# A two-layer decoder trunk on one core: last token tile by column halves, third tile's last pass on two other engines, queries ahead of values, and the values' copy ahead of an exponential

## The chip, the cores and the metric

The kernel runs on one core of a Trainium2 chip. The metric is the device time of one execution in microseconds (us), lower is better. The core has TensorE (PE in the rows; PEld is its weight load), VectorE (DVE), ScalarE (ACT), GpSimd (POOL) and the queue of SyncE (SP), which issues nearly all DMAs. The engines run side by side and wait for each other through semaphores; each engine takes its own instructions strictly in the order written.

## The reference, cut to what matters

The trunk has a layer of native sparse attention (NSA) and one of forgetting attention (FoX), each followed by a gated MLP. `x` is 512 tokens by 1024. Every sub-layer ends in a layer norm over the 1024 columns of a token:

```python
def layer_norm(x, g, b):
    mu = jnp.mean(xf, axis=-1, keepdims=True)
    var = jnp.mean(jnp.square(xf - mu), axis=-1, keepdims=True)
    y = (xf - mu) * lax.rsqrt(var + LN_EPS)
    return y * g + b
...
x = layer_norm(ALPHA * x + y, ln1_g[i], ln1_b[i])
f = conv_ffn(x, ffn_w_up[i], ffn_conv_w[i], ffn_conv_b[i], ffn_w_down[i])
x = layer_norm(ALPHA * x + f, ln2_g[i], ln2_b[i])
```

NSA projects 16 heads of queries in 4 groups. Each group has keys and values of 64 columns for a "selected" and a "window" branch, and rotary (`apply_rope`) on queries and keys, not on values. A third branch attends to 31 compressed blocks. FoX is causal attention with an additive bias, 16 heads, handled in 8 pairs.

## The kernel before, in words

Each product is made of three: both operands are split into a high and a low part, and PE does high by high, high by low and low by high. A weight chunk comes by DMA into one of four `raw` slots; ScalarE makes its high part (`hi`), GpSimd the low part (`lo`), then PE may use it.

**NSA items.** A group's projections are four items of eight steps (`kstep`): n = 4 * group + k with k = 0 keys, 1 values, 2 queries of the first head pair, 3 queries of the second. All four go through bank BP of PSUM (the eight 512-column accumulator banks `ps`), which ScalarE empties by `item_copy`. Keys and queries then pass the rotary: the SP queue swaps halves by four DMAs (`swap_halves`), GpSimd multiplies by cosine, VectorE by sine (`item_dve`), GpSimd adds, ScalarE makes the high part (`item_hi`), GpSimd the low one (`rope_lo`), and for queries the SP queue moves both into place (`move_queries`). `double_keys` copies the keys to the other partitions. Values are instead turned by PE through bank BX (`values_turn`), which compressed scores (`cmp_scores`) and compressed probabilities (`cmp_turn`) use too.

The first group's items stand in a prologue, one after another, among the last steps of the compression (`cmp_hidden`, the `vcs` copies, the first compressed softmax `cmp_mask` to `cmp_scale`). Then follow 4 groups of 32 units, u = 32 * g + v. A unit is one query block of one head and branch: scores, `unit_max` (VectorE), `unit_exp` (ScalarE), scaling (GpSimd), transpose (PE), `unit_hi` and `unit_lo` (ScalarE and VectorE), product with values. While group g runs, the items of group g + 1 are projected, one step per unit, and an item's rotary lies in the eight units behind its projection. The order is written out by hand on each engine.

**FoX.** `fox_stages` runs eight units per head pair, with the next pair's three projections between them. In the last unit ScalarE copies the next pair's values out of bank BP (`fox_value_copy`), and PE needs that bank for the pair after it.

**The end.** The down projection writes tile m (128 tokens) into banks 2m and 2m + 1, and the last four weight chunks are done tile by tile (`down_pe`). `ln_dve` and `tile_std` then do for each tile: residual in two halves (L1635), mean (L1638), squares on ScalarE over all 1024 columns (L795), square root (L798), scaled by gain (L1645), inverse (L1648), last pass in two halves (L1652). Two DMAs store each tile.

## Time and profile before

| | us |
|---|---|
| three runs, median | 1373.08 |
| lowest and highest run | 1370.35, 1373.63 |
| the profiled execution, its own time | 1374.31 |
| its span in the trace | 1372.5 |
| TensorE matmuls busy in it | 1322.0 (96%) |
| VectorE, ScalarE, GpSimd busy | 635.4, 674.6, 599.4 |

The span runs from the first to the last event of the core; some 1.8 us of the execution lie outside it. An engine's busy time says how full it is, not whether it sets the end: for that one reads who waits for whom.

### The profile page before, as it was taken

To read this page: it belongs to the slowest core of one execution; us is meant where nothing else is said; L and a number is where in the kernel's file an instruction comes from. 1 tells how busy PE (TensorE), PEld (TensorE's weight loads), DVE (VectorE), ACT (ScalarE), POOL (GpSimd) and SP (SyncE) were. 2 spreads that over 40 slices of the span, in tenths; PEclk is the share of its full clock that TensorE was granted. 3 is DMA by queue.
4 is the path that set the end of the run, shared out by engine and by line. 5 is a ranking of instruction groups with operands and counts; after the bars stand their busy time and mean duration, and the time that the engine had idled before them with its cause. 6 is when DMAs were issued, how large, how long until landed. Compare 5 with 4: busy or idle time off the path is not lost.

```text
span 1372.5 us, 19855 instructions
## 1 busy us (share of the span) xinstructions
PE 1322.0 (96%) x6858; PEld 1108.3 (81%) x6858; DVE 635.4 (46%) x1469; ACT 674.6 (49%) x1257; POOL 599.4 (44%) x399
## 2 busy tenths in 40 slices
PE   8979999979999999999999999998999999999997
PEld 6868887867898888888888788887898888888885
DVE  3347777775544433440006767768354343341005
ACT  4347777765444444442214767776354444443122
POOL 2267767763434444444444222222244444444441
PEclk9999999999999999999999999999999999999999
DMA  9442322222323333334333321322424333334321
GB/s 296 108 102 61 85 70 78 69 70 97 99 82 108 92 95 103 92 105 131 101 92 95 87 62 49 94 64 62 154 78 123 92 92 98 100 93 137 103 66 62
DMA packets 172798, 131.98 MB, mean 96 GB/s; under 512 B 24544, under 2 KB 156244, under 8 KB 172724
## 3 DMA queue, kind: packets, MB, share of 16 engines
q1 hardware_dynamic: 172724, 131.02, 33.0%
q8 instruction: 43, 0.70, 0.2%
q14 instruction: 31, 0.25, 0.1%
HBM read 117.17 MB, written 4.39 MB: 89 GB/s over the span
## 4 chain that ended last, share of the span: by engine, by line
PE 82%; DVE 5%; issue 4%; ACT 4%; POOL 2%; DMA 2%; SPq 1%; DVEq 0%; POOLq 0%; ACTq 0%
PE ps L964 15%; PE ps L965 15%; PE ps L966 15%; PE ps L1218 7%; PE ps L1221 7%; PE ps L1219 7%; PE ps L1124 3%; PE ps L1138 2%; PE ps L1091 2%; PE ps L1264 2%; PE ps L1260 2%; PE ps L1259 2%; DVE ptl L1507 1%; DVE prob L1489 1%; PE ps L1137 1%
## 5 line engine op out<-in xcount | busy, mean ns | idle before, releaser
L488 POOL TENSOR_TENSOR wl<-raw,wh 128x1024 fp32r<-128x1024 f32 x178 | 426.3, 2398 | 648.0 <-ACT wh L611 647.9
L964 PE MATMUL ps<-xh,wh 128*128 128x512 f32 x968 | 381.8, 394 | 4.2 <-ACT work L900 3.9
L965 PE MATMUL ps<-xl,wh 128*128 128x512 f32 x968 | 377.9, 390 | 0.0
L966 PE MATMUL ps<-xh,wl 128*128 128x512 f32 x968 | 377.4, 390 | 0.0
L611 ACT ACTIVATE wh<-raw 128x1024 fp32r<-128x1024 f32 x192 | 201.2, 1050 | 191.8 <-PE ps L1221 182.2
L964 PEld LDWEIGHTS ps<-xh,wh 128*128 128x128 f32 x968 | 182.2, 188 | 41.9 <-ACT work L900 5.8
L966 PEld LDWEIGHTS ps<-xh,wl 128*128 128x128 f32 x968 | 181.9, 188 | 38.8
L965 PEld LDWEIGHTS ps<-xl,wh 128*128 128x128 f32 x968 | 182.1, 188 | 33.4
L1664 DVE SCALAR_TENSOR_TENSOR work<-ps,conv,work 128x511 f32<-128x511 f32 x88 | 66.0, 750 | 222.0 <-ACT work L847 156.7
L705 ACT ACTIVATE prob<-prob,negmax 128x128 f32<-128x128 f32 x192 | 107.4, 559 | 69.4 <-DVE negmax L1489 67.5
L1218 PE MATMUL ps<-wh,gh 128*128 128x512 f32 x352 | 137.1, 390 | 0.0
L1219 PE MATMUL ps<-wl,gh 128*128 128x512 f32 x352 | 136.9, 389 | 0.0
L1635 DVE SCALAR_TENSOR_TENSOR ps<-xt,ps 128x512 f32<-128x512 f32 x32 | 21.4, 710 | 237.9 <-PE ps L1221 237.9
L1489 DVE CUSTOM_DVE_ANT_0 prob<-ps,seen 128x128 f32<-128x128 f32 x192 | 92.8, 484 | 42.7 <-PE ps L1344 29.6
L1221 PE MATMUL ps<-wh,gl 128*128 128x512 f32 x352 | 108.4, 389 | 0.0
L548 POOL TENSOR_SCALAR prob<-prob,rinv,gate 128x128 f32<-128x128 f32 (+3 forms) x128 | 78.7, 615 | 65.9 <-DVE rinv L1496 64.2
L712 ACT ACTIVATE pth<-ps 128x128 fp32r<-128x128 f32 x192 | 82.3, 429 | 43.4 <-PE ps L1124 42.2
L1507 DVE TENSOR_TENSOR ptl<-ps,pth 128x128 fp32r<-128x128 f32 x192 | 93.1, 485 | 3.9 <-ACT pth L712 3.4
L1124 PE MATMUL ps<-ident,prob 128*128 128x128 f32 x480 | 87.3, 280 | 6.4 <-POOL prob L548 3.2
L850 ACT ACTIVATE gh<-work 128x512 f32 (+1 forms) x44 | 27.8, 632 | 118.5 <-DVE work L1676 118.5
L1221 PEld LDWEIGHTS ps<-wh,gl 128*128 128x128 f32 x352 | 66.1, 188 | 13.8
L1218 PEld LDWEIGHTS ps<-wh,gh 128*128 128x128 f32 x352 | 66.1, 188 | 13.7
(197 smaller groups left out, 1948.8 us busy)
## 6 DMA issues: line engine op xcount, KB each, us to landing
raw<-in_ffn_w_up SPq DMA_DIRECT2D x88, 512.0 KB, 3.8
raw<-in_ffn_w_down SPq DMA_DIRECT2D x44, 512.0 KB, 3.6
raw<-in_fox_w_in SPq DMA_DIRECT2D x24, 512.0 KB, 4.0
raw<-in_nsa_w_in SPq DMA_DIRECT2D x12, 512.0 KB, 4.9
xt<-in_x SPq DMA_DIRECT2D x8, 512.0 KB, 5.0
raw<-in_nsa_w_in SPq DMA_DIRECT2D x16, 256.0 KB, 3.8
qs<-work SPq DMA_DIRECT2D x32, 128.0 KB, 2.3
raw<-in_nsa_w_o SPq DMA_DIRECT2D x8, 512.0 KB, 4.1
```

The source lines that it names most:

```text
L488: nc.gpsimd.tensor_tensor(wl[:, slot, :, :], raw[:, slot, :, :], wh[:, slot, :, :].bitcast(F32), ALU.subtract).then_inc(s_wl, 1)
L611: nc.scalar.activation(wh[:, slot, :, :], raw[:, slot, :, :], ACT.Copy).then_inc(s_wh, 1)
L705: nc.scalar.activation(prob[:, u % 3, 0:n], prob[:, u % 3, 0:n], ACT.Exp, bias=negmax[:, b:b + 1], scale=-1.0, accum_out=psumrow[:, b:b + ...
L964: nc.tensor.matmul(o, ah, bh, start=start, stop=False)
L965: nc.tensor.matmul(o, ah, bl, start=False, stop=False)
L966: return nc.tensor.matmul(o, al, bh, start=False, stop=stop)
L1124: last = nc.tensor.transpose(ps[:, BT + u % 2, kt * P:(kt + 1) * P], prob[:, u % 3, kt * P:(kt + 1) * P], ident[:, :])
L1218: nc.tensor.matmul(ps[:, 2 * m + h, :], a_h, hi_w[:, cs], start=start, stop=False)
L1219: nc.tensor.matmul(ps[:, 2 * m + h, :], a_h, lo_w[:, cs], start=False, stop=False)
L1221: last = nc.tensor.matmul(ps[:, 2 * m + h, :], a_l, hi_w[:, h * 512:(h + 1) * 512], start=False, stop=stop)
L1489: nc.vector.tensor_tensor_reduce(out=prob[:, u % 3, 0:n], in0=ps[:, BS + u % 2, 0:n], in1=seen[:, SEQ - n:SEQ], scale=-1.0, scalar=3e38, o ...
L1507: nc.vector.tensor_tensor(turned_blocks(ptl, i), ps[:, BT + u % 2, 0:(i + 1) * P].rearrange("p (k c) -> p k c", c=P), turned_blocks(pth, i ...
```

## The change

1. The item order within a group becomes keys, first queries, values, second queries (`KIND`); waits on counters follow it, and the values' turn, high part and low part move to units 25, 26 and 27.
2. The prologue is reordered on PE, ScalarE, VectorE, GpSimd and SP alike.
3. In FoX the values' copy stands ahead of the exponential of the same unit on ScalarE.
4. In the last layer norm the fourth tile is projected by column halves, and its variance is put together from the squares of each half about its own mean and the gap between the two means. The third tile's last pass is made by ScalarE (times the inverse) and GpSimd (plus `b_row`) in place of VectorE.

```diff
+KIND = (0, 2, 1, 3)
...
+        def rotated_ahead(n):
+            return n - (n + 1) // 4
         def queries_ahead(n):
-            return 2 * (n // 4) + max(n % 4 - 2, 0)
+            return 2 * (n // 4) + n % 4 // 2
...
-                if n % 4 == 3 or n % 4 == 0 and n:
+                if n % 4 == 2 or n % 4 == 0 and n:
                     move_queries(n - 1)
-                if n % 4 == 1:
+                if n % 4 == 1 and n > 1:
                     double_keys(n // 4)
-                else:
+                if n % 4 != 2:
                     swap_halves(n)
+                if n == 1:
+                    double_keys(0)
             def load_item(n):
-                g, k, c = n // 4, n % 4, 4 + n
+                g, k, c = n // 4, KIND[n % 4], 4 + n
                 if k >= 2:
                     load(c, c % R, cols(w_nsa, g * REP * HD + (k - 2) * P))
...
-                sp.wait_ge(s_y, 3 * QT + n + 1)
+                if m == 2:
+                    sp.wait_ge(s_yp, half + 1)
+                else:
+                    sp.wait_ge(s_y, 3 * QT + (n if m < 2 else n - 2) + 1)
...
+            for h in range(2):
+                cs = slice(h * 512, (h + 1) * 512)
+                pool.wait_ge(s_yr, h + 1)
+                nc.gpsimd.tensor_tensor(xt[:, 2, cs], xt[:, 2, cs], b_row[:, cs], ALU.add).then_inc(s_yp, 1)
...
-                    if turned and w == (3, 5, 2, 2)[item[1]]:
+                    if turned and w == (3, 2, 2, 2)[item[1]]:
                         item_hi(*item)
...
                 for v in range(8):
+                    if more and v == 7:
+                        fox_value_copy(C_FOX + 3 * (pair + 1) + 2, NSA_ITEMS + 3 * (pair + 1))
                     if more or v + 2 < 8:
                         unit_exp(U + v + 2, (v + 2) % 4)
-                    if more and v == 7:
-                        fox_value_copy(C_FOX + 3 * (pair + 1) + 2, NSA_ITEMS + 3 * (pair + 1))
...
-            for m in range(QT):
+            for m in range(QT - 1):
                 tile_std(3, m)
+            act.wait_ge(s_lt, 1)
+            act.wait_ge(s_sq, 4 * QT - 1)
+            nc.scalar.activation(swapped.bitcast(BF16)[:, 0:512], ps[:, 6, :], ACT.Square, bias=last_mean[:, 0:1],
+                                 accum_out=squares[:, 3:4]).then_inc(s_sq, 1)
+            act.wait_ge(s_rstd, 4 * QT - 1)
+            act.wait_ge(s_gz, 4 * QT - 1)
+            for h in range(2):
+                nc.scalar.activation(xt[:, 2, h * 512:(h + 1) * 512], ps[:, 4 + h, :], ACT.Identity, scale=rstd[:, 2:3],
+                                     bias=zero[:, 0:1]).then_inc(s_yr, 1)
+            act.wait_ge(s_lt, 3)
+            act.wait_ge(s_sq, 4 * QT)
+            nc.scalar.activation(swapped.bitcast(BF16)[:, 512:1024], ps[:, 7, :], ACT.Square, bias=last_mean[:, 1:2],
+                                 accum_out=second_squares[:, :]).then_inc(s_sq, 1)
+            act.wait_ge(s_lt, 6)
+            act.wait_ge(s_sq, 4 * QT + 1)
+            nc.scalar.activation(std[:, 3:4], second_squares[:, :], ACT.Sqrt, bias=last_var[:, 0:1], scale=1.0 / D).then_inc(s_std, 1)
...
-            pe.wait_ge(s_kc, 3)
-            item_steps(0)
-            conv_turn(0)
-            cmp_hidden(1)
-            pe.wait_ge(s_kc, 4)
-            item_steps(1)
-            pe.wait_ge(s_gel, 2)
-            for g in range(GROUPS):
-                for hb in range(2):
-                    last = nc.tensor.matmul(ps[0:NCMP, 4, g * HD:(g + 1) * HD], ghid[:, hb, g * NCMP:(g + 1) * NCMP], w2v[:, hb, :],
-                                            start=(hb == 0), stop=(hb == 1))
-            last.then_inc(s_cmpo, 1)
-            pe.wait_ge(s_pl, 1)
-            values_turn(0)
-            item_steps(2)
-            conv_turn(1)
...
+                    pe.wait_ge(s_pl, 4 * g + 2 + h // 2 * 2)
                     pe.wait_ge(s_qm, 64 * (2 * g + 1 + h // 2))
...
+                n = 4 * ((H + 1) // 4) + 3
+                if H and n < NSA_ITEMS:
                     pe.wait_ge(s_pl, n)
...
+                pe.wait_ge(s_pf, 4 * g + 2 + j % 2 * 2)
...
+                if not j:
+                    pe.wait_ge(s_pl, 3)
                 for i in range(QT):
...
+                if p % 16 == 0:
+                    pe.wait_ge(s_pl, 4 * g + 3)
                 pv(p, bank, vv[g % 2][:, :, br, :, :], p % 4 == 0, p % 4 == 3)
...
+            pe.wait_ge(s_kc, 3)
+            item_steps(0)
+            conv_turn(0)
+            item_steps(1)
+            cmp_hidden(1)
+            pe.wait_ge(s_kc, 4)
+            item_steps(2)
+            pe.wait_ge(s_gel, 2)
+            for g in range(GROUPS):
+                for hb in range(2):
+                    last = nc.tensor.matmul(ps[0:NCMP, 4, g * HD:(g + 1) * HD], ghid[:, hb, g * NCMP:(g + 1) * NCMP], w2v[:, hb, :],
+                                            start=(hb == 0), stop=(hb == 1))
+            last.then_inc(s_cmpo, 1)
             pe.wait_ge(s_cmpr, 1)
             cmp_scores(0)
-            item_steps(3)
+            conv_turn(1)
+            item_steps(3, 0, 4)
+            pe.wait_ge(s_cmask, 1)
+            values_turn(0)
+            item_steps(3, 4)
...
-                    if v == 19 and g < GROUPS - 1:
+                    if v == 25 and g < GROUPS - 1:
                         pe.wait_ge(s_cl, u // 16 + 1)
                         values_turn(g + 1)
...
+                        if m == QT - 1 and not turn_banks:
+                            last = down_half(c0 + k, k, m, 0, src_h, src_l, at, False, k == nk - 1)
+                            continue
                         last = down_product(c0 + k, k, m, src_h, src_l, at, False, k == nk - 1)
                         if m == QT - 1:
                             last.then_inc(s_wu, 1)
-                    if m < QT - 1:
+                    if m < QT - 1 or not turn_banks:
                         last.then_inc(s_zt, 1)
+                if not turn_banks:
+                    for k in range(nk - R, nk):
+                        down_half(c0 + k, k, QT - 1, 1, src_h, src_l, at, False, k == nk - 1).then_inc(s_wu, 1)
...
+            cmp_mask(0)
+            cmp_difference(0)
+            conv_copy(1)
             item_dve(0, 2)
-            conv_copy(1)
-            for step in (cmp_mask, cmp_difference, cmp_sum, cmp_inverse, cmp_gate, cmp_scale):
+            for step in (cmp_sum, cmp_inverse, cmp_gate, cmp_scale):
                 step(0)
...
-                    if turned and w == (6 if item[1] == 1 else 1):
+                    if turned and w == (3 if item[1] == 2 else 1):
                         item_dve(*item)
...
+            def residual(m, h):
+                cs = slice(h * 512, (h + 1) * 512)
+                nc.vector.scalar_tensor_tensor(out=ps[:, 2 * m + h, :], in0=xt[:, m, cs], scalar=ALPHA, in1=ps[:, 2 * m + h, :],
+                                               op0=ALU.mult, op1=ALU.add, accum_out=zsum[:, m, h:h + 1]).then_inc(s_z, 1)
+            def half_scaled(m, h):
+                cs = slice(h * 512, (h + 1) * 512)
+                return nc.vector.scalar_tensor_tensor(out=ps[:, 2 * m + h, :], in0=ps[:, 2 * m + h, :], scalar=negmean[:, m:m + 1],
+                                                      in1=g_row[:, cs], op0=ALU.add, op1=ALU.mult)
+            def last_tiles():
+                t2, t3 = 4 * QT - 2, 4 * QT - 1
+                dve.wait_ge(s_zt, 3 * (QT - 1) + 3)
+                dve.wait_ge(s_y, 2 * QT + 3)
+                residual(2, 0)
+                residual(2, 1)
+                dve.wait_ge(s_z, 2 * t2 + 2)
+                nc.vector.tensor_scalar(negmean[:, 2:3], zsum[:, 2, 0:1], zsum[:, 2, 1:2], -1.0 / D, ALU.add, ALU.mult).then_inc(s_mv, 1)
+                dve.wait_ge(s_zt, 3 * (QT - 1) + 4)
+                dve.wait_ge(s_y, 2 * QT + 4)
+                residual(3, 0)
+                dve.wait_ge(s_z, 2 * t3 + 1)
+                nc.vector.tensor_scalar(last_mean[:, 0:1], zsum[:, 3, 0:1], -2.0 / D, None, ALU.mult).then_inc(s_lt, 1)
+                dve.wait_ge(s_mv, t2 + 1)
+                dve.wait_ge(s_sq, t2 + 1)
+                half_scaled(2, 0)
+                half_scaled(2, 1).then_inc(s_gz, 1)
+                dve.wait_ge(s_std, t2 + 1)
+                nc.vector.reciprocal(rstd[:, 2:3], std[:, 2:3]).then_inc(s_rstd, 1)
+                dve.wait_ge(s_sq, t3 + 1)
+                nc.vector.tensor_scalar(first_var[:, :], squares[:, 3:4], 1.0 / D, EPS, ALU.mult, ALU.add).then_inc(s_lt, 1)
+                dve.wait_ge(s_wu, C_END)
+                residual(3, 1)
+                dve.wait_ge(s_z, 2 * t3 + 2)
+                nc.vector.tensor_scalar(last_mean[:, 1:2], zsum[:, 3, 1:2], -2.0 / D, None, ALU.mult).then_inc(s_lt, 1)
+                dve.wait_ge(s_lt, 3)
+                nc.vector.tensor_scalar(half_gap[:, :], last_mean[:, 0:1], last_mean[:, 1:2], 0.5, ALU.subtract, ALU.mult).then_inc(s_lt, 1)
+                nc.vector.tensor_scalar(negmean[:, 3:4], last_mean[:, 0:1], last_mean[:, 1:2], 0.5, ALU.add, ALU.mult).then_inc(s_lt, 1)
+                dve.wait_ge(s_lt, 4)
+                nc.vector.scalar_tensor_tensor(out=last_var[:, :], in0=half_gap[:, :], scalar=half_gap[:, 0:1], in1=first_var[:, :],
+                                               op0=ALU.mult, op1=ALU.add).then_inc(s_lt, 1)
+                dve.wait_ge(s_lt, 5)
+                half_scaled(3, 0)
+                dve.wait_ge(s_sq, t3 + 2)
+                half_scaled(3, 1).then_inc(s_gz, 1)
+                dve.wait_ge(s_std, t3 + 1)
+                nc.vector.reciprocal(rstd[:, 3:4], std[:, 3:4]).then_inc(s_rstd, 1)
+                dve.wait_ge(s_gz, t3 + 1)
+                dve.wait_ge(s_rstd, t3 + 1)
+                for h in range(2):
+                    cs = slice(h * 512, (h + 1) * 512)
+                    nc.vector.scalar_tensor_tensor(out=xt[:, 3, cs], in0=ps[:, 6 + h, :], scalar=rstd[:, 3:4], in1=b_row[:, cs],
+                                                   op0=ALU.mult, op1=ALU.add).then_inc(s_y, 1)
...
-                for m in range(QT):
+                for m in range(QT if banks else 2):
...
             ln_dve(3, C_END, None)
+            last_tiles()
```

Left out are declarations, the reordering of ScalarE's prologue (its rows stand below), GpSimd's (rotary of the first queries ahead of the eighth and ninth low parts), and the same two substitutions (`KIND[...]` for the item's kind, `rotated_ahead` for the count of rotated items) wherever an item is handled.

On ScalarE in the prologue, from the second compression step's activation (`ghid`) on, this stood before (`qf` is the queries' copy, `work<-ps` the copy of keys or values, `vv` the values' high part, `vcs` the compressed values, `csm` the compressed softmax):

```order
L650 ACTIVATE ghid<-ps,vecs 128x124 [waits cmp_out,vectors_ready,cmp_hidden]
L650 ACTIVATE ghid<-ps,vecs 128x124
L698 ACTIVATE ks<-work 64x512 [waits rope_sum]
L698 ACTIVATE kw<-work 64x512
L683 ACTIVATE work<-ps 128x512 [waits proj_lo,w_used]
L611 ACTIVATE wh<-raw 128x1024 [waits w_used,raw_landed0]
L741 ACTIVATE vcs<-ps 31x256 [waits cmp_out]
L741 ACTIVATE vcs<-ps 31x256 x3
L691 ACTIVATE vv<-ps 128x8x64 [waits proj_turned]
L685 ACTIVATE qf<-ps 128x512 [waits w_used]
L611 ACTIVATE wh<-raw 128x1024 [waits w_used,raw_landed1]
L695 ACTIVATE work<-work 128x512 [waits rope_sum]
```

and this stands from the queries' copy on now:

```order
L707 ACTIVATE qf<-ps 128x512 [waits w_used]
L720 ACTIVATE ks<-work 64x512 [waits rope_sum]
L720 ACTIVATE kw<-work 64x512
L633 ACTIVATE wh<-raw 128x1024 [waits w_used,raw_landed0]
L672 ACTIVATE ghid<-ps,vecs 128x124 [waits cmp_out,vectors_ready,cmp_hidden]
L672 ACTIVATE ghid<-ps,vecs 128x124
L717 ACTIVATE work<-work 128x512 [waits rope_sum]
L705 ACTIVATE work<-ps 128x512 [waits proj_lo,w_used]
L765 ACTIVATE vcs<-ps 31x256 [waits cmp_out]
L765 ACTIVATE vcs<-ps 31x256 x3
L753 ACT_TABLE_LOAD
L753 ACTIVATE csm<-csm 128x256 [waits cmp_differences]
```

The queries' copy and their rotary now come ahead of the values' copy and of `vcs`; the table load and the exponential of `csm` come ahead of the values' high part.

On ScalarE in the seventh and eighth unit of the first FoX pair before:

```order
L611 ACTIVATE wh<-raw 128x1024 [waits w_used,raw_landed1]
L705 ACTIVATE prob,psumrow<-prob,negmax 128x128 [waits neg_max]
L712 ACTIVATE pth<-ps 128x3x128 [waits pv_done,probs_turned]
L722 ACTIVATE work<-ps 64x512 [waits o_summed,pv_done]
L705 ACTIVATE prob,psumrow<-prob,negmax 128x256 [waits neg_max]
L900 ACTIVATE work<-ps 128x512 [waits proj_lo,w_used]
L712 ACTIVATE pth<-ps 128x4x128 [waits pv_done,probs_turned]
L705 ACTIVATE prob,psumrow<-prob,negmax 128x384 [waits neg_max]
```

and now (L922 is the values' copy, L727 the exponential):

```order
L633 ACTIVATE wh<-raw 128x1024 [waits w_used,raw_landed1]
L727 ACTIVATE prob,psumrow<-prob,negmax 128x128 [waits neg_max]
L734 ACTIVATE pth<-ps 128x3x128 [waits pv_done,probs_turned]
L744 ACTIVATE work<-ps 64x512 [waits o_summed,pv_done]
L922 ACTIVATE work<-ps 128x512 [waits proj_lo,w_used]
L727 ACTIVATE prob,psumrow<-prob,negmax 128x256 [waits neg_max]
L734 ACTIVATE pth<-ps 128x4x128 [waits pv_done,probs_turned]
L727 ACTIVATE prob,psumrow<-prob,negmax 128x384 [waits neg_max]
```

The copy moved up by one row.

On VectorE at the end of the program, the fourth tile before:

```order
L1635 SCALAR_TENSOR_TENSOR ps,zsum<-xt,ps 128x512 [waits tile_normed,w_used]
L1635 SCALAR_TENSOR_TENSOR ps,zsum<-xt,ps 128x512
L1638 TENSOR_SCALAR negmean<-zsum 128x1 [waits tile_sums]
L1645 SCALAR_TENSOR_TENSOR ps<-ps,negmean,work 128x1024 [waits tile_squares]
L1648 RECIPROCAL rstd<-std 128x1 [waits tile_std]
L1652 SCALAR_TENSOR_TENSOR xt<-ps,rstd,work 128x512 [waits tile_inverse,tile_scaled]
L1652 SCALAR_TENSOR_TENSOR xt<-ps,rstd,work 128x512
```

and now, from the third tile's inverse on (its own residual, the first residual half of tile four with its mean, and the third tile's scaling stand ahead of it):

```order
L1706 RECIPROCAL rstd<-std 128x1 [waits tile_std]
L1708 TENSOR_SCALAR first_var<-squares 128x1 [waits tile_squares]
L1678 SCALAR_TENSOR_TENSOR ps,zsum<-xt,ps 128x512 [waits w_used]
L1712 TENSOR_SCALAR last_mean<-zsum 128x1 [waits tile_sums]
L1714 TENSOR_SCALAR half_gap<-last_mean 128x1 [waits last_tile_steps]
L1715 TENSOR_SCALAR negmean<-last_mean 128x1
L1717 SCALAR_TENSOR_TENSOR last_var<-half_gap,first_var 128x1 [waits last_tile_steps]
L1684 SCALAR_TENSOR_TENSOR ps<-ps,negmean,work 128x512 [waits last_tile_steps]
L1684 SCALAR_TENSOR_TENSOR ps<-ps,negmean,work 128x512 [waits tile_squares]
L1724 RECIPROCAL rstd<-std 128x1 [waits tile_std]
L1729 SCALAR_TENSOR_TENSOR xt<-ps,rstd,work 128x512 [waits tile_inverse,tile_scaled]
L1729 SCALAR_TENSOR_TENSOR xt<-ps,rstd,work 128x512
```

The third tile's last pass is gone from VectorE, half of the fourth tile's residual has moved ahead, and four one-column instructions stand between its second half and its scaling.

## Rows read from the trace of the kernel before

**Rows 1.** The page: busy us of engines; one group: busy, mean ns | idle before.
```profile
PE 1322.0 (96%) x6858; PEld 1108.3 (81%) x6858; DVE 635.4 (46%) x1469; ACT 674.6 (49%) x1257; POOL 599.4 (44%) x399
...
L611 ACT ACTIVATE wh<-raw 128x1024 fp32r<-128x1024 f32 x192 | 201.2, 1050 | 191.8 <-PE ps L1221 182.2
```

**Rows 2.** Waits of PE, whole span: us in total, times, longest.
```profile
PE ps L1138 <- DVE ptl L1507: 14.7, 18, 2.9
PE ps L1091 <- DMA qs<-work: 4.7, 1, 4.7
PE ps L964 <- ACT work L900: 3.9, 6, 0.7
...
PE ps L1091 <- issue: 1.9, 3, 0.7
```

**Rows 3.** Timeline, prologue's end: start, us, engine line op, [idle <-releaser].
```profile
58.27 2.95 SPq L381 DMA_DIRECT2D raw<-in_nsa_w_in  x4
...
71.14 1.26 POOL L532 TENSOR_TENSOR kw<-work,kw 64x512 fp32r<-64x512 f32 x1 [0.17 <-POOL ks L532]
72.48 4.75 POOL L488 TENSOR_TENSOR wl<-raw,wh 128x1024 fp32r<-128x1024 f32 x2
...
88.16 2.34 POOL L488 TENSOR_TENSOR wl<-raw,wh 128x1024 fp32r<-128x1024 f32 x1
...
74.08 1.51 ACT L741 ACTIVATE vcs<-ps 31x256 fp32r<-31x256 f32 x4
...
76.93 1.69 DVE L1566 TENSOR_TENSOR vcs<-ps,vcs 31x256 fp32r<-31x256 f32 x4
...
89.19 1.33 DVE L1549 TENSOR_TENSOR cstat<-cstat,gate 128x8 f32<-128x8 f32 x1
...
91.89 0.29 DVE L1489 CUSTOM_DVE_ANT_0 prob<-ps,seen 128x128 f32<-128x128 f32 x1 [0.91 <-PE ps L1091]
```

**Rows 4.** Busy by stretches of us: PE, PEld, DVE, ACT, POOL (x), PEclk, DMA.
```profile
93.00:94.40 1.40, 1.40 (x6) 1.00 (x5) 0.63 (x3) 0.71 (x3) 1.19 (x3) 0.50 0.42 102
```

**Rows 5.** Timeline, inside the NSA groups, VectorE and PE.
```profile
280.40 0.69 DVE L1481 TENSOR_TENSOR work<-work,sinT 128x512 f32<-128x512 f32 x1 [3.07 <-DMA work<-qf]
...
143.08 0.36 PE L1138 MATMUL ps<-pth,vv 128*128 128x256 f32 x1 [0.73 <-DVE ptl L1507]
...
281.85 0.35 PE L1138 MATMUL ps<-pth,vv 128*128 128x256 f32 x1 [2.85 <-DVE ptl L1507]
```

**Rows 6.** The chain that ended last, one FoX pair: start, us, what.
```profile
812.33 0.49 ACT prob L705 x2
...
812.84 0.61 ACT work L900
...
813.49 0.51 PE ps L964
```

**Rows 7.** Timeline, the same FoX pair.
```profile
811.42 1.93 DVE L1503 TENSOR_SCALAR prob<-prob,rinv 128x128 f32<-128x128 f32 x1
...
814.81 0.15 DVE L1496 RECIPROCAL rinv<-psumrow 128x1 f32<-128x1 f32 x1
...
810.88 2.38 POOL L488 TENSOR_TENSOR wl<-raw,wh 128x1024 fp32r<-128x1024 f32 x1 [6.89 <-ACT wh L611]
```

**Rows 8.** Timeline, the last products and the fourth tile.
```profile
1362.68 0.61 PE L1221 MATMUL ps<-wh,gl 128*128 128x512 f32 x2
...
1364.24 0.69 DVE L1635 SCALAR_TENSOR_TENSOR ps<-xt,ps 128x512 f32<-128x512 f32 x1
...
1367.15 1.29 DVE L1645 SCALAR_TENSOR_TENSOR ps<-ps,negmean,work 128x1024 f32<-128x1024 f32 x1 [1.27 <-ACT work L795]
...
1368.62 1.41 DVE L1652 SCALAR_TENSOR_TENSOR xt<-ps,rstd,work 128x512 f32<-128x512 f32 x2
```

**Rows 9.** Timeline, an earlier layer norm with GpSimd at work.
```profile
375.02 0.22 DVE L1638 TENSOR_SCALAR negmean<-zsum 128x1 f32<-128x1 f32 x1
...
367.54 9.48 POOL L488 TENSOR_TENSOR wl<-raw,wh 128x1024 fp32r<-128x1024 f32 x4 [16.85 <-ACT wh L611]
```

63 lines of the change are left out of this document (34 added, 29 removed).

## The prediction

> **What bounds the kernel now.** I read the page first: TensorE is busy for 1322 of 1372.5 us [rows 1], so nothing but its some 50 us of idle time can be won by an order of work, and none of the edits takes a product away. Next the waits of TensorE, to see where these 50 us lie: 14.7 us in 18 waits for a transposed probability's low part, one wait of 4.7 us for moved queries, six waits for the FoX values' copy with 3.9 us, three "issue" waits of 0.6 each, at the first score of a new NSA group [rows 2]. The rest is the start and the end, where TensorE is done at 1363.29 and the fourth tile's layer norm runs alone on VectorE and ScalarE [rows 8]. Last I read the timeline around each of these places for what was late.
>
> **The end.** Tile four's residual begins at 1364.24, though its products end at 1362.68 + 0.61 = 1363.29: VectorE is still in tile three's last pass. Its last pass begins at 1368.62, 4.38 us after its residual [rows 8]. Now VectorE does tile three's residual, then the first half of tile four's (its products are there at about 1360.6, an estimate: twelve of the tile's 24 remain, and two take 0.61 with 0.39 for the second's run-out, so 0.22 from one to the next), then tile three's scaling. By 0.69 for each half [rows 8] and 0.2 for each one-column instruction [rows 9] it is free at about 1363.2, so the second half starts with the products, at 1363.33: 0.91 earlier. Behind it: residual half and its accumulator 0.83, four one-column instructions of 0.2 to 0.25, a third of that overlapping, 0.7; scaling in two halves 1.3, inverse and hop 0.25. That makes 3.1; the squares of the second half (half of tile-wide ones, some 0.7) and the root lie beside the scaling. Before it was 4.38. I add 0.2 for a port (below): last pass at 1366.65 in place of 1368.62, a gain of **2.0**. Behind that pass both kernels have the same two stores. The third tile's path on ScalarE (two copies, 0.6 each) and GpSimd (two additions of 1.3, as for the keys [rows 3]) ends near 1366.3, ahead of tile four's first store at 1367.4. If the small steps cost double, 1.0 of the gain is left; without port and overlap losses it is 2.3.
>
> The port: GpSimd's chunk held up VectorE's two-input instruction on 8 columns, which took 1.33 and ended with the chunk at 88.16 + 2.34 = 90.50 [rows 3], and a scaling of 128 columns, 1.93 long, to 813.35, GpSimd's end being 813.26 [rows 7]. A one-column instruction (L1638) beside GpSimd's chunks took 0.22 as ever [rows 9]. Of the four new small ones only `last_var` has two tensors in SBUF. It is due at about 1364.7, within GpSimd's first addition (1363.7 to 1365.0). One wait to its end costs 0.2 to 0.3, which I take; if GpSimd's second addition goes ahead of it, 1.3 more. The Trainium skill ("SBUF — State Buffer", "Who interferes with whom") says that a VectorE instruction with two SBUF inputs contends with a GpSimd one that reads SBUF, and that the one that begins first holds the port for its whole length. The trace agrees for 8 columns; no row shows one column with two inputs. By the rule and a lost turn the end would gain 0.7, not 2.0: rival C.
>
> **FoX.** ScalarE makes an exponential from 812.33 on (0.49) and only then the values' copy, 812.84 to 813.45; TensorE resumes at 813.49 [rows 6]. The copy's product is long there. With the copy first it ends at 812.94, and TensorE, which has its scores to 812.85, waits 0.1 at most. The exponential comes 0.6 later, at 813.4; its first user on VectorE stands at 814.81, behind a scaling that GpSimd's chunk holds to 813.35 [rows 7]. So it is covered by 1.4; were that gone, the copy's gain would turn up again as a wait of up to 0.6 for the inverse. Six waits of 0.65 become six of 0.05: **3.6**, bounds 2.4 and 3.9.
>
> **The prologue.** One wait is replaced by another here. Before: the first queries' rotary lies behind the values, and TensorE stands 4.7 for their move; the first unit's maximum is at 91.89 [rows 2, 3]. Now the first queries are projected second. I follow the chain from the keys' low part. It ended at 72.40 [rows 3] and comes 0.74 earlier, since SP has three load issues, not four (2.95 for four), ahead of the keys' swap: 71.66. Then on GpSimd a chunk of 2.4, cosine and sum of 1.3 each (by the keys' 1.26), to 76.65; ScalarE's high part 0.65, GpSimd's low one 1.3: 78.6. The move's four DMAs then land by 82. ScalarE's values copy (0.61 [rows 6]), held by that low part: 79.3; `vcs` 1.5 on it and 1.7 on VectorE: 82.5; three VectorE steps and the exponential at 0.4 each, by the quarter of `vcs` [rows 3]: 84.3. Its table load has run since 80.8. A chunk's high part 1.05 [rows 1] and the values' 0.6 on ScalarE: 85.9; their low part on VectorE 0.7; sum and inverse 0.6: 87.2. The gate then stands, as it did, for GpSimd's chunk, from 85.3 to 87.6, scaling to 88.1, first maximum at 88.15. Gain **3.7**. TensorE: three items of 5.5 and 7.2 for the compression end at 76, small work 78, a wait to 79.3 for the values' copy, half an item, a wait for the mask from 82.0 to 82.9, the rest to 86.2; so it is 2 us ahead of the maximum and not the bound. TensorE ran at half its clock in the first units (0.50, that is 1.2 GHz, behind 4.7 us of standing [rows 2, 4]). With shorter gaps that may go: 0 to 1.0 more, I take 0. If a link costs 0.2 more at each of the ten hand-overs, 2 us are lost: bounds 1.7 and 4.7.
>
> **The groups.** The three "issue" waits go, since the first queries of a group are now moved eight units, some 15 us, earlier: 1.9 [rows 2]. The rotary of the queries now falls in units 16 to 23 in place of 24 to 31. There VectorE stands for the swap's DMA as it did (3.07 in one case, and TensorE 2.85 behind it where it has no projection to do [rows 5]), but next to `cmp_scale` and `cmp_lo` in place of the compressed softmax; queued behind it are the maxima and low parts, and ScalarE and GpSimd wait for these. In units 24 to 31 one wait of 0.73 [rows 5] goes. The values' low part now falls in unit 27 and `cmp_scores` in 28 waits for it. I put the waits saved at 0.7 and the new ones at three of 0.5: net **1.1**, bounds -2 and 3. The values' turn has no partner to wait for. The loads moved in SP's queue are issued two items ahead and cost nothing; without that lead issue and landing would stand open as the swap's do, some 3 us.
>
> **Sum.** 2.0 + 3.6 + 3.7 + 1.1 = 10.4. Against the profiled execution, 1374.31, that is 1363.9. The runs' median is 1.2 lower, so I predict 1373.08 - 10.4 = **1362.7**.
>
> **Rivals.**
> - A, all as above: 1362.7, own range 1360 to 1365.5. Chance 0.66.
> - B, the groups give back: the swap's wait at unit 17 with the blocked `cmp_scale`, and `cmp_scores` behind the values, cost TensorE 1.5 more in each group. For it speaks the 2.85 above, against it that this one stood in group 3, where no projections fill in. 10.4 - 4.5 = 5.9: 1367.2. Chance 0.15.
> - C, the port takes 1.3 of the end: 1364.0. Chance 0.12.
> - D, no change: the change doesn't do what it says. The copy's gain returns as a late exponential (0) and the prologue's chain is as late as before (0), which leaves 3.1: 1370.0. Against it speak the cover of 1.4 and the 3.7 in the chain. Chance 0.05.
> - E, slower: one mechanism, at unit 28 of three groups. `cmp_scores` stands in front of all of TensorE's work and waits for the values' low part, that for ScalarE, that for the turn on TensorE two units earlier. For a slower kernel that circle must cost over 9.3 + 4.1 = 13.4 in three groups (without the 1.1), 4.5 each, more than two units. The longest wait of this sort was 2.85 [rows 5]. At 5 each: 1378.8. Chance 0.02.
>
> **The numbers.** A measurement of this kernel tells some 0.3%, 4.1 us, from no change: faster is below 1369.0. A, B and C are faster, D is the same, E slower; with some of D's and B's spread: 0.92, 0.06, 0.02. The range holds A, C and B: 1359 to 1368, the low end by the upper bounds of two terms and the clock's 1.0.
>
> **What would show it.** First maximum near 88.2 and no wait for moved queries. The three "issue" waits gone, waits in units 17 to 20 under 1 us each, none over 0.5 at the compressed scores of unit 28. The six waits for the FoX copy at 0.1 or gone, the pairs 0.6 shorter. Tile four's second residual half at 0.05 behind the last product, last pass 3.3 behind it, `last_var` below 0.5. Wrong would be: a first maximum after 90, new waits of TensorE for the exponential in FoX, or `last_var` over 1 us.

## The result and the profile after

| | before | after |
|---|---|---|
| median of five runs, us | 1373.12 | 1363.18 |
| lowest and highest | 1370.35, 1374.93 | 1360.90, 1365.69 |
| span of the profiled execution | 1372.5 | 1361.4 |

The change makes the kernel faster: the ratio is 0.993, its 95% interval 0.9911 to 0.9948, so 7 to 12 us are gained, 9.9 by the medians. The forecast was 1362.7. That the sum came out within 0.5 us doesn't mean that its terms did: two errors of opposite sign met, and most of what follows is about them.

The page after, and the waits of TensorE over the whole span, beside [rows 1, 2]:

```profile
PE 1322.4 (97%) x6858; PEld 1106.7 (81%) x6858; DVE 632.1 (46%) x1475; ACT 676.1 (50%) x1261; POOL 603.9 (44%) x401
```

```profile
PE ps L1162 <- DVE ptl L1559: 13.4, 20, 2.1
PE ps L1019 <- DMA xt<-in_x: 4.7, 3, 3.0
PE ps L1148 <- POOL prob L566: 3.8, 7, 0.8
PE ps L1002 <- ACT work L705: 2.0, 2, 1.7
...
PE ps L1002 <- ACT work L922: 1.0, 6, 0.2
PE ps L1112 <- DVE negmax L1541: 0.8, 1, 0.8
```

The wait for moved queries and the three "issue" waits are gone, and the six for the FoX copy have 1.0 us in place of 3.9. TensorE now waits 0.8 for the first maximum, and 1.7 of the 2.0 on L705 for the values' copy in the prologue, as worked out ahead. The three waits for `in_x` at the very start are 1.2 longer (4.7 for 3.5): an input landed later, which the change doesn't touch.

VectorE at the end of the prologue (start, duration, instruction):

```profile
89.38 0.38 DVE L1601 TENSOR_TENSOR cstat<-cstat,gate 128x8 f32<-128x8 f32 x1 [0.28 <-DVE cstat L1594]
89.79 0.42 DVE L1606 TENSOR_TENSOR csm<-csm,cstat 128x256 f32<-128x256 f32 x1
90.14 0.28 DVE L1541 CUSTOM_DVE_ANT_0 prob<-ps,seen 128x128 f32<-128x128 f32 x1
```

GpSimd's chunk in front of it:

```profile
87.33 2.40 POOL L507 TENSOR_TENSOR wl<-raw,wh 128x1024 fp32r<-128x1024 f32 x1 [4.23 <-ACT wh L633]
```

The gate takes 0.38, not 1.33 [rows 3]. GpSimd's chunk held it all the same, only for less time: the gate ends at 89.76 and the chunk at 89.73 (before at 90.52 and 90.50), while in a run below, where the chunk was all but done, it took 0.17. The first maximum is at 90.14, against 91.89. But the first item's copy stands at 58.35, against 57.13, so from copy to maximum it is 31.79 in place of 34.76.

The end, TensorE and then VectorE, beside [rows 8]:

```profile
1353.55 0.39 PE L1003 MATMUL ps<-wl,gh 128*128 128x512 f32 x1
1353.78 0.39 PE L1004 MATMUL ps<-wh,gl 128*128 128x512 f32 x1
```

```profile
1354.20 0.70 DVE L1678 SCALAR_TENSOR_TENSOR ps<-xt,ps 128x512 f32<-128x512 f32 x1 [0.34 <-PE ps L1004]
...
1355.43 0.55 DVE L1717 SCALAR_TENSOR_TENSOR last_var<-half_gap,first_var 128x1 f32<-128x1 f32 x1
1355.91 1.40 DVE L1684 SCALAR_TENSOR_TENSOR ps<-ps,negmean,work 128x512 f32<-128x512 f32 x2
1357.23 0.15 DVE L1724 RECIPROCAL rstd<-std 128x1 f32<-128x1 f32 x1
1357.48 1.41 DVE L1729 SCALAR_TENSOR_TENSOR xt<-ps,rstd,work 128x512 f32<-128x512 f32 x2
```

The products end at 1354.17, the second residual half begins 0.03 behind them and the last pass 3.31 behind them. Before it was 5.33.

To see where the 11.1 us between the two spans lie, I cut both traces at marks that any kernel here has: the first item's copy on ScalarE, the first maximum, the first residual of each layer norm (LN0 to LN3), and the end of the last product. These are differences of start times in the timeline of each profile, in us:

```
                         before   after   gained
start to first copy       57.13   58.35    -1.22
first copy to maximum     34.76   31.79     2.97
maximum to LN0 (groups)  260.67  255.94     4.73
LN0 to LN1 (first MLP)   364.52  365.61    -1.09
LN1 to LN2 (FoX)         265.42  260.39     5.03
LN2 to LN3 (second MLP)  364.51  365.65    -1.14
LN3 to last product       16.28   16.44    -0.16
last product to the end     9.2     7.2      2.0
```

Three rows are not as forecast: the groups gained 4.7 and not 1.1, FoX 5.0 and not 3.6, and both MLPs lost 1.1, where no edit had been costed at all. The experiments go after these.

### The profile page after: what moved, and what is told of

Same layout as the page of the kernel before. It is cut to its first block, busy times and chain, and to the rows that moved or that the text cites. A ratio compares the mean times of both kernels' runs of the same rounds, so it can differ in the third digit from the quotient of the medians.

```text
span 1361.4 us, 19872 instructions
## 1 busy us (share of the span) xinstructions
PE 1322.4 (97%) x6858; PEld 1106.7 (81%) x6858; DVE 632.1 (46%) x1475; ACT 676.1 (50%) x1261; POOL 603.9 (44%) x401
## 4 chain that ended last, share of the span: by engine, by line
PE 81%; DVE 5%; POOL 4%; issue 4%; ACT 4%; DMA 1%; SPq 1%; DVEq 0%; POOLq 0%; ACTq 0%
PE ps L1002 15%; PE ps L1004 15%; PE ps L1003 15%; PE ps L1264 7%; PE ps L1263 7%; PE ps L1266 7%; PE ps L1148 2%; PE ps L1162 2%; PE ps L1315 2%; PE ps L1311 2%; PE ps L1310 2%; POOL prob L566 1%; DVE ptl L1559 1%; DVE prob L1541 1%; PE ps L1112 1%
## 5 line engine op out<-in xcount | busy, mean ns | idle before, releaser
L727 ACT ACTIVATE prob<-prob,negmax 128x128 f32<-128x128 f32 x192 | 107.4, 559 | 60.1 <-DVE negmax L1541 57.8
L1264 PEld LDWEIGHTS ps<-wl,gh 128*128 128x128 f32 x344 | 64.6, 188 | 13.9
## 6 DMA issues: line engine op xcount, KB each, us to landing
raw<-in_nsa_w_in SPq DMA_DIRECT2D x16, 256.0 KB, 3.8
```

The source lines that it names most:

```text
L727: nc.scalar.activation(prob[:, u % 3, 0:n], prob[:, u % 3, 0:n], ACT.Exp, bias=negmax[:, b:b + 1], scale=-1.0, accum_out=psumrow[:, b:b + ...
L1264: nc.tensor.matmul(ps[:, 2 * m + h, :], a_h, lo_w[:, cs], start=False, stop=False)
```

## Experiments

Each run below is compared with the kernel before by a ratio with its 95% interval, three single executions apart; the same marks are read from its profile.

### One part alone

Kernel before, only the FoX copy:

```diff
+                    if more and v == 7:
+                        fox_value_copy(...)
                     if more or v + 2 < 8:
                         unit_exp(U + v + 2, (v + 2) % 4)
-                    if more and v == 7:
-                        fox_value_copy(...)
```

> The kernel before, with only the values' copy ahead of the exponential in FoX. Theory 1 (the prediction's term, at the size that the trace after shows): the six waits of 0.65 us become six of 0.16, six pair spacings shrink from 25.24 to 24.75 us, the time falls by 2.9 us; no new wait of TensorE for a late exponential. Theory 2 (rival D): the exponential's lateness comes back, the pair spacing stays at 25.24 and the time falls by 0. Theory 3: the whole 5.0 us by which FoX got shorter belongs to this edit (then the last pair too must lose its half-clock stretch by it), the time falls by 5.0.

Measured: 0.9963 (0.9949 to 0.9977). The six waits are 0.16 each:

```profile
793.87 0.50 PE L964 MATMUL ps<-xh,wh 128*128 128x512 f32 x1 [0.16 <-ACT work L900]
818.62 0.50 PE L964 MATMUL ps<-xh,wh 128*128 128x512 f32 x1 [0.16 <-ACT work L900]
```

The pairs are 24.75 apart in place of 25.24: 6 x 0.49 = 2.9 by the trace, and theory 2 is out. The ratio says 5.1 us, at least 3.2, which is more than these 2.9; where the rest lies no profile shows. (The one profiled execution is the slowest of the twelve, and its copy-to-maximum stretch is 3.6 us longer than before, though no edit is there.) What the profiles do show is why FoX got shorter by 5.0 in the table. In FoX's last pair, which the edit doesn't touch, stand two rows of VectorE and GpSimd, of the kernel before and then of the kernel with items only (below):

```profile
946.96 2.49 DVE L1503 TENSOR_SCALAR prob<-prob,rinv 128x128 f32<-128x128 f32 x1
947.00 2.38 POOL L488 TENSOR_TENSOR wl<-raw,wh 128x1024 fp32r<-128x1024 f32 x1 [1.09 <-ACT wh L611]
```

```profile
937.61 0.29 DVE L1516 TENSOR_SCALAR prob<-prob,rinv 128x128 f32<-128x128 f32 x1
937.66 2.48 POOL L495 TENSOR_TENSOR wl<-raw,wh 128x1024 fp32r<-128x1024 f32 x1 [1.12 <-ACT wh L617]
```

VectorE's scaling begins just ahead of GpSimd's chunk. Over all fourteen profiles of this study the lead decides: with 0.03 to 0.04 us (31 to 43 ns, nine profiles) the scaling takes 2.49 to 2.51 and ends 0.08 to 0.09 behind the chunk, and TensorE later waits 1.25 and 0.82; with 0.05 to 0.06 (50 to 62 ns, five profiles) it takes 0.29 and TensorE waits 0.2 to 0.3. Whether the edit is there has no part in it: of the five profiles with it three were lost, of the nine without it six. The price shows between the kernel with the late rotary (below; lost, FoX 264.08) and that with items only (won, 261.99), which have the same FoX instructions and no half clock there: 2.1. FoX's 5.03 in the table are 2.9 from the edit and 2.1 from this place, which was lost in the profile of before and won in that of after; each of the two also has 3.4 us at half clock in FoX (behind 952 and 764), and these cancel. Theory 3 is out: in the edit's own profile the last pair is as it was, lost place included.

Kernel before, only the last layer norm (the fourth tile by column halves, `last_tiles`, the third tile's pass on ScalarE and GpSimd; the diff is that of the change).

> The kernel before, with only the last layer norm changed. Theory 1: the last pass of tile four begins 3.3 us behind the last product in place of 5.3, the time falls by 2.0 us, and last_var takes about 0.55. Theory 2 (rival C, a lost turn at the port): last_var takes 1.3 or more in some execution, the last pass begins 4.6 behind the last product, the time falls by 0.7.

Measured: 1.0007 (0.9989 to 1.0024), no gain, at most 1.5 us. Yet the place itself behaves: products end at 1364.46, last pass at 1367.77, 3.31 behind, `last_var` 0.56, and from the last product to the end 7.2 in place of 9.2. Theory 1 holds for the place, not for the time: the gain of 2.0 is there and is given back, by the marks in the MLPs: 365.59, 365.62 and 16.45, all three as in the changed kernel. So the loss of 2.4 belongs to this edit; a run further below says how.

The change without these two edits, and without the six small tensors:

```diff
+                    if more or v + 2 < 8:
+                        unit_exp(U + v + 2, (v + 2) % 4)
                     if more and v == 7:
                         fox_value_copy(...)
-                    if more or v + 2 < 8:
-                        unit_exp(U + v + 2, (v + 2) % 4)
...
-            last_tiles()
```

> The change without its edits to FoX and the last layer norm: item order and prologue alone. Theory 1 (the prediction): first maximum 3.7 us earlier, groups 1.1 shorter, time falls by 4.8. Theory 2 (from the two traces): measured from the first item's copy the first maximum comes 3.0 earlier, and from there to the first layer norm 4.7 us are gained, 1 to 1.5 by waits and about 3 by TensorE's granted clock, which stood at 0.50 for some 7 us behind a wait of 2.85 in the last group before; the time falls by 6.5 to 7.5. Theory 3 (rival B): each group gives back 1.5, the time falls by 0.3 to 2.

Measured: 0.9946 (0.9928 to 0.9964), some 7.4 us. Copy to maximum 31.84, maximum to LN0 253.79. Theory 2 fits the time and the prologue; the groups gained more than its 4.7 in this profile, 6.9. Theory 3 is out. The ratios of the three parts add up to more than the whole change brings (5.1 - 1.0 + 7.4 against 9.6), but each is uncertain by some 2 us.

The same, with the old item order in the groups behind the first:

```diff
-KIND = (0, 2, 1, 3)
+KINDS = ((0, 2, 1, 3),) + ((0, 1, 2, 3),) * 3
...
-                    if v == 25 and g < GROUPS - 1:
+                    if v == 19 and g < GROUPS - 1:
```

> As the run before it, but the items of the other three groups stay in the order keys, values, first and second queries, with the values' turn in unit 19; only the first group has the new order and the new prologue. Theory 1 (clock): the wait of 2.85 us in the last group is back and TensorE's clock falls to 0.50 behind it for some 7 us, so from the first maximum to the first layer norm it takes about 260 us as before, and the time falls by 3.0 to 3.7 only, 3.5 to 4.5 less than with the order in all groups. Theory 2 (the prediction's sizes): the groups' order is worth 1.1, the time falls by 3.7. The granted clock in the last group tells the two apart: 0.50 for 7 us, or 1.00 with the wait there.

Measured: 0.9966 (0.995 to 0.9982), some 4.7 us (2.5 to 6.9), which tells no theory from another. Copy to maximum 32.70, maximum to LN0 257.53. The "issue" waits are back, and the waits of TensorE from behind the first maximum to the first layer norm are, with the old order and then with the new one:

```profile
PE ps L1131 <- DVE ptl L1521: 11.6, 16, 1.8
PE ps L1117 <- POOL prob L555: 3.6, 6, 0.8
PE ps L1081 <- issue: 1.9, 3, 0.7
```

```profile
PE ps L1130 <- DVE ptl L1520: 10.1, 18, 1.4
PE ps L1116 <- POOL prob L554: 3.6, 6, 0.8
```

17.1 against 13.7: the groups' order gives 3.4 of the 3.7 by which this stretch differs, 3.3 by the medians (1368.83 and 1365.53). The intervals of the two ratios overlap, and the stretch took 255.0 to 256.0 in the three other profiles with the new order and no half clock in it, so 1.6 to 3.7 is the careful figure. Of it 1.9 are the "issue" waits. Some 1.0 is the wait in the last group, which is 1.77 here and 0.82 there but varies from execution to execution in both orders (0.86 to 2.85 in the old one, 0.82 to 2.07 in the new). The clock theory fell by the sign that I had named: a wait was there, though of 1.77 and not 2.85, and the clock stayed at 1.00.

### Half clock

In the profile of before the granted clock stood at its lower level (1.2 GHz) in three stretches, in that of after in two, the end apart, where TensorE has no work left. The windows (PE, PEld, DVE, ACT, POOL, granted clock, DMA), before and then after:

```profile
283.00:290.00 7.00, 5.93 (x21) 4.23 (x20) 4.74 (x15) 5.36 (x13) 5.61 (x8) 0.51 0.32 75
952.00:956.00 4.00, 3.65 (x17) 3.37 (x18) 3.18 (x10) 1.86 (x5) 0.00 (x0) 0.57 0.06 23
91.90:95.30 3.40, 3.40 (x10) 2.62 (x10) 1.67 (x9) 2.08 (x7) 2.09 (x3) 0.51 0.36 85
```

```profile
82.00:86.00 4.00, 4.00 (x13) 3.11 (x12) 3.07 (x8) 2.13 (x4) 1.10 (x1) 0.58 0.70 155
764.00:768.00 4.00, 3.86 (x13) 2.91 (x12) 3.36 (x11) 3.96 (x10) 2.08 (x1) 0.58 0.94 228
283.00:290.00 7.00, 5.97 (x41) 4.73 (x41) 5.14 (x22) 5.33 (x18) 5.59 (x9) 1.00 0.25 75
```

At half clock TensorE does half the products (21 against 41 in the same 7 us), so a stretch of 7 us costs up to 3.4. These pieces last 3.4 or 6.8 us. What one of 3.4 costs shows in FoX, where the kernels before and with the late rotary (below) have the same instructions: 265.41 with the piece behind 952, 264.08 without it, 1.3 us. Over all profiles of this study one place is regular: with the old prologue a piece began in or right behind the wait of 4.7 for moved queries, 0.1 to 3.2 us ahead of the first maximum, in all eight; with the new one in none of six, though in three of them a piece began earlier, at 80.4 to 81.9. In three of the eight old ones another piece began at 74.7 to 77.9, and these have the longest way from copy to maximum (36.8 to 38.6, the other five 34.8 to 35.3). The pieces behind 283 and 952 come and go between kernels that are the same there. That behind 764, some 50 us into FoX, came in all four profiles whose tensors lie 192 bytes further (see below) and in none of the five whose tensors stand where they stood (at the other shifts in three of five); that the place brings it is not shown.

The wait in the last group was attacked directly, in the kernel before:

```diff
-                    if turned and w == (6 if item[1] == 1 else 1):
+                    if turned and w == (2 if item == (3, 3) else (6 if item[1] == 1 else 1)):
                         item_dve(*item)
...
-                    if turned and w == 2:
+                    if turned and w == (3 if item == (3, 3) else 2):
                         rope_sum(*item)
```

and likewise one unit later for its `item_hi` and `rope_lo`.

> The kernel before, with the last item's rotary (second queries of the last group, in units 0 to 7 of that group) one unit later on VectorE, GpSimd and ScalarE. TensorE there waited 1.5 to 2.9 us in the profiles with the order of before, 0.8 to 2.1 with the new one, behind VectorE, which stands for the swap's DMA; in two of three profiles its clock was 0.50 for 6.8 us behind it. Theory 1 (the stand for the DMA is the cause): the wait near 190 us behind the first maximum falls below 1, no half clock there, and the stretch from the first maximum to the first layer norm falls to 255 to 257 us from 258.6 to 261.8; the time falls by 2 to 4. Theory 2 (the wait moves on to the maxima of the next unit): the stretch stays at 258 or more.

Measured: 0.9991 (0.998 to 1.0001), no measurable gain. The wait is shorter but a second one stands behind it:

```profile
282.53 0.30 PE L1124 MATMUL ps<-ident,prob 128*128 128x128 f32 x1 [1.07 <-DVE ptl L1507]
284.42 0.58 PE L1138 MATMUL ps<-pth,vv 128*128 128x256 f32 x1 [1.11 <-DVE ptl L1507]
```

The stretch took 258.19, and a piece of 3.4 us at half clock followed all the same. That is theory 2, with a part of theory 1: the stand moved on by one unit. What decides whether the clock falls there stays open: over all profiles it fell behind 2.85 and 2.50, but also behind 1.6 and behind these two of 1.1, and not behind others of 1.5 to 2.1.

### Both halves of the end

The changed kernel with tile three's last pass on VectorE again:

```diff
                 nc.vector.reciprocal(rstd[:, 2:3], std[:, 2:3]).then_inc(s_rstd, 1)
+                for h in range(2):
+                    cs = slice(h * 512, (h + 1) * 512)
+                    nc.vector.scalar_tensor_tensor(out=xt[:, 2, cs], in0=ps[:, 4 + h, :], scalar=rstd[:, 2:3], in1=b_row[:, cs],
+                                                   op0=ALU.mult, op1=ALU.add).then_inc(s_yp, 1)
```

> The changed kernel, but tile three's last pass is on VectorE again, ahead of the second residual half of tile four; ScalarE and GpSimd have no part in it. Theory 1 (both halves of the edit are needed): VectorE is busy with the pass for 1.3 us, so that the second residual half begins about 0.8 behind the last product in place of 0.03, and the last pass 4.1 less 0.35 (no GpSimd at last_var, 0.2 in place of 0.55), 3.8 behind the last product in place of 3.3; the time rises by 0.5. Theory 2 (the column halves carry the gain alone): last pass at 3.3 or earlier.

Measured: 0.9945 (0.993 to 0.996). Products end at 1355.62; on VectorE:

```profile
1355.37 1.41 DVE L1702 SCALAR_TENSOR_TENSOR xt<-ps,rstd,work 128x512 f32<-128x512 f32 x2
1356.70 0.15 DVE L1705 TENSOR_SCALAR first_var<-squares 128x1 f32<-128x1 f32 x1
1356.76 0.69 DVE L1669 SCALAR_TENSOR_TENSOR ps<-xt,ps 128x512 f32<-128x512 f32 x1
...
1357.98 0.22 DVE L1714 SCALAR_TENSOR_TENSOR last_var<-half_gap,first_var 128x1 f32<-128x1 f32 x1
...
1359.69 1.41 DVE L1726 SCALAR_TENSOR_TENSOR xt<-ps,rstd,work 128x512 f32<-128x512 f32 x2
```

The second residual half is 1.14 late and the last pass 4.07 behind the products: 0.76 more than with the moved pass, where 0.5 was expected. So the column halves give 1.3 of the 2.0, the moved pass 0.8: theory 1. The whole time is less clear. The median is 1367.20, 6.4 below the kernel before, where the changed kernel is 9.9 below it; the intervals of the two ratios overlap, and 0.8 of the difference is what the end accounts for. `last_var` takes 0.22 here, with GpSimd idle, and 0.55 beside GpSimd's addition, which in the changed kernel ends at 1355.97, `last_var` at 1355.99:

```profile
1354.71 1.26 POOL L614 TENSOR_TENSOR xt<-xt,work 128x512 f32<-128x512 f32 x1 [18.89 <-ACT xt L988]
```

### The down projection's one per cent

In the first MLP neither instructions nor their order differ between the two kernels, yet it took 1.1 us longer. The groups of TensorE's products over 75 us of its down projection, changed kernel:

```profile
L1264 PE MATMUL ps<-wl,gh 128*128 128x512 f32 x110 | 43.2, 393 | 0.0
L1263 PE MATMUL ps<-wh,gh 128*128 128x512 f32 x110 | 42.9, 390 | 0.0
L1266 PE MATMUL ps<-wh,gl 128*128 128x512 f32 x109 | 33.9, 391 | 0.0
```

Before, each had a mean of 389 ns over the same 75 us, and there was no idle time in either:

```profile
L1219 PE MATMUL ps<-wl,gh 128*128 128x512 f32 x111 | 43.2, 389 | 0.0
```

The edit declares six small tensors; each takes 32 bytes of a partition, so all that is declared behind them, `gh` and `gl` among it, lies 192 bytes further. Kernel before, with nothing but that:

```diff
+        pad = sb("pad", [P, 48])
         table = sb("table", [P, 1])
```

> The kernel before with one unused tensor of 192 bytes per partition where the change has its six new one- and two-column tensors; no instruction differs. In the kernels with the new layer norm each MLP took 365.6 us in place of 364.5, all of it in the down projection, where six products took 1.373 in place of 1.365 us, also in the first MLP, whose instructions the change doesn't touch. Theory 1 (place in SBUF): the tensors behind the new ones, among them both operands gh and gl of the down projection, lie 192 bytes further; each MLP takes 365.6 again, the last 72 products 16.45 in place of 16.28, and the time rises by 2.3. Theory 2 (TensorE's longer program, fetched differently): MLPs at 364.5, no change.

Measured: 0.9998 (0.9986 to 1.001); the MLPs take 365.64 and 365.59, the last products 16.44. By the marks theory 1 holds to 0.05 us in all three places, and theory 2 is out: no instruction differs. The whole time rose by 0.6, not 2.3, and the interval ends at 1.4. In the profile the loss has nothing to hide behind, as TensorE is never idle there; that something else in this kernel gains 1 us or more I can neither show nor exclude. So the loss is shown by the marks, and its full size in the whole time is not, in this run. By the starts of all products of the down projection in this profile six take 1.373 us against 1.360 before, so my 1.365 was a little high.

Changed kernel, moved on to 256 bytes, and with `last_var` of one tensor and two one-column scalars:

```diff
+        pad = sb("pad", [P, 16])
         table = sb("table", [P, 1])
...
-                nc.vector.scalar_tensor_tensor(out=last_var[:, :], in0=half_gap[:, :], scalar=half_gap[:, 0:1], in1=first_var[:, :],
-                                               op0=ALU.mult, op1=ALU.add).then_inc(s_lt, 1)
+                nc.vector.tensor_scalar(last_var[:, :], half_gap[:, :], half_gap[:, 0:1], first_var[:, 0:1], ALU.mult, ALU.add).then_inc(s_lt, 1)
```

> The changed kernel with an unused tensor of 64 bytes more, so that gh, gl and the rest stand 256 bytes behind their place of before, and with the variance's instruction (last_var) as one tensor with two one-column scalars in place of two tensors. Place in SBUF, theory 1: each MLP takes 364.5 again and the time falls by 2.3 against the changed kernel. Theory 2 (the program's length): 365.6 stays. Port, theory 1: last_var falls from 0.55 to about 0.2 us and the last pass begins 3.0 behind the last product in place of 3.3; theory 2 (it waits for something other than the port, as the two semaphores in front of it): it stays at 0.55. Both first theories: 2.6 us below the changed kernel, some 12 below the kernel before.

Measured: 0.9903 (0.9888 to 0.9919), 1360.85, 2.3 below the changed kernel's median (2.8 when each is held against its own runs of the kernel before; the intervals overlap a little). The MLPs are at 364.54 and 364.54. The products of the down projection and the variance:

```profile
L1264 PE MATMUL ps<-wh,gh 128*128 128x512 f32 x111 | 43.2, 389 | 0.0
L1265 PE MATMUL ps<-wl,gh 128*128 128x512 f32 x111 | 43.2, 389 | 0.0
L1267 PE MATMUL ps<-wh,gl 128*128 128x512 f32 x110 | 33.8, 389 | 0.0
```

```profile
1354.07 0.27 DVE L1718 TENSOR_SCALAR last_var<-half_gap,first_var 128x1 f32<-128x1 f32 x1
...
1355.83 1.41 DVE L1729 SCALAR_TENSOR_TENSOR xt<-ps,rstd,work 128x512 f32<-128x512 f32 x2
```

The last pass is 3.03 behind the last product (1352.80). Both first theories hold by the marks. The six tensors and the pad together move the operands by 256 bytes.

Which places are good? The kernel before with a pad of 8, 16 and 32 columns (32, 64 and 128 bytes), one execution each, beside which the kernel before had a median of 1373.48:

> The kernel before with 32 unused bytes per partition in the place of the earlier 192: gh and gl lie 32 bytes further (both began at a multiple of 128 or 64 bytes before: gh 138880, gl 183936). Theory 1 (what counts is the place within 64 bytes): slow here, MLPs at 365.6, and the shift by 192 slow for another reason. Theory 2 (within 128 bytes): slow here too, MLPs at 365.6 or more. Theory 3 (which tensors share a larger stretch): 364.5.

> As before, 64 unused bytes. Theory 2 (place within 128 bytes): as with 192 bytes, MLPs at 365.6 and the last 72 products at 16.45. Theory 1 (within 64 bytes): 364.5 and 16.28.

> As before, 128 unused bytes. Theory 2 (place within 128 bytes): MLPs at 364.5, the last 72 products at 16.28. If slow, the place within 256 bytes counts, for which the shift by 256 of the run with the changed kernel (364.54) speaks as well.

```
bytes moved by     0       32      64      128     192     256
first MLP, us      364.52  367.84  367.83  367.36  365.6   364.54
second MLP         364.51  367.80  367.82  367.32  365.6   364.54
last 72 products    16.28   16.76   16.75   16.70   16.44   16.28
one execution              1383.68 1382.65 1375.90
```

All three are worse than 192, so my theories of 64 and of 128 bytes are both wrong, and the third too. Only 0 and 256 are undisturbed, and the loss isn't the same in between. The first product of the down projection came 260.9 to 261.3 us behind the layer norm in all, so the up projections, which read other tensors, took the same to 0.3 us. From one product of the down projection to the next it is 226.7 ns at 0 and 256, 228.9 at 192, 232.4 at 128 and 233.3 at 32 and 64: up to 2.9% more. A product of the down projection by shift 128:

```profile
L1219 PE MATMUL ps<-wh,gh 128*128 128x512 f32 x109 | 43.0, 395 | 0.0
L1220 PE MATMUL ps<-wl,gh 128*128 128x512 f32 x108 | 42.6, 394 | 0.0
L1222 PE MATMUL ps<-wh,gl 128*128 128x512 f32 x108 | 33.9, 395 | 0.0
```

Last, the changed kernel with 64 bytes more, the one-tensor variance and the late rotary of the last group:

> The changed kernel with the three edits that gained: 64 more unused bytes, last_var with one tensor, the last group's rotary one unit later. If the late rotary's gain of 1 us adds to the others, 1359.9, some 1 below the run without it and 13.5 below the kernel before (ratio 0.990); if the unit behind takes it back, 1360.9 (0.991).

Measured: 0.9905 (0.9885 to 0.9926), 1360.84, the same as without the late rotary. By the marks the groups take 255.01 in place of 254.97: two waits of 1.29 and 1.11 stand where one of 1.77 and one of 1.28 stood. The unit behind takes it back.

## Why the prediction was right, and where its terms were not

**The end, 2.0.** Right, in its place and size (2.0 in the last stretch), and by its own steps: residual half 0.03 behind the products, last pass 3.31 behind them, 3.3 having been forecast, `last_var` waiting 0.3 for the port. Rival C, a lost turn, was seen in neither profile with this form of `last_var` and GpSimd beside it (0.55 and 0.56). What the step left out is what the edit does elsewhere: the term priced the edit's instructions, and its six tensors at nothing. These cost 2.4 us in the two MLPs and the last products, more than the edit brings, and by itself it gains nothing (1.0007). No view of the profile before shows this, and none of my rivals had it.

**FoX, 3.6.** The mechanism was right, the size was not: the waits fell to 0.16, not 0.05, so the term is 2.9 by the trace, within its bounds (the ratio would allow more). No exponential was late; rival D's return of 0.6 per pair is refuted by the spacing of 24.75. The other 2.1 us of FoX in the two profiles are the last pair's scaling that got through ahead of GpSimd's chunk: a lead longer by 0.02 us, so luck.

**The prologue, 3.7.** 2.97 by the two profiles, 3.3 by the medians of all (35.2 in eight with the old prologue, 31.9 in six with the new). The chain ran as worked out, up to the gate that ends with GpSimd's chunk. The 0.8 that is missing had come by the first queries' low part: it ended 22.3 us behind the first copy, 21.5 having been worked out. Half of that is the keys' swap: its DMAs were issued 1.15 earlier, counted from the copy, but VectorE's sine began 5.60 behind the first issue where it was 4.85 before, so 0.4 was gained and not 0.74. The other half is GpSimd's next chunk (2.72 for 2.4) and the steps between. Its sign "a first maximum after 90" did occur (90.14), because the start itself was 1.22 later; it should have been given against the first copy. The term that I had taken as 0 within 0 to 1.0, the clock in the first units, was mis-sized: the fall at the 4.7 us was there in all eight old prologues, with 3.4 or 6.8 us at half clock, and in none of six new ones. That alone is up to 1.7 or 3.4, and the one piece whose price shows cost 1.3 for 3.4 us. It counts in the stretch behind the maximum, and so do the groups below.

**The groups, 1.1.** Mis-sized. The isolated comparison gives 3.7 by the trace and 3.3 by the medians; without the one wait that varies, 2.8. The "issue" waits gave their 1.9. What failed is "the new ones at three of 0.5": the new waits near units 17 to 20 are one in each of three groups, of 0.19 to 0.36 in the five profiles with the new order, and none at the compressed scores. Rival B (1.5 lost per group) and rival E are out. From copy to LN0 the old order took 293.4 to 300.1 in eight profiles, the new one 285.6 to 289.4 in five, so items and prologue together are the largest part of the gain, where I had FoX and prologue alike.

**The sum.** Forecast 2.0 + 3.6 + 3.7 + 1.1 = 10.4. By the isolated stretches 2.0 + 2.9 + 3.0 + 3.7 - 2.4 = 9.2, and some return of the clock; measured 9.9. The groups brought more than was forecast, which hid the loss in the MLPs. That these two errors cancelled is luck, and rival A had the right time partly for the wrong reasons.

## What to carry to other kernels

Cut two traces at marks that both have and compare stretch by stretch, the untouched ones above all: here they held the largest surprise. A new small tensor moves all that is declared behind it; check that the mean duration of the products hasn't changed, and if it has, try a pad (64 bytes more gave the 2.4 us back here). And a wait of 1 to 5 us on TensorE may cost its clock as well, so the price of such a wait is its length and, where the clock falls, up to half of the slow stretch behind it.
